# Recurrence heads of a two-block layer: the next head's first exponential and mixed operands made at the end of a head, and a longer first projection

## The reference, cut to what matters

```python
def hgrn2_forget(f_raw, lb):
    f = lb + (1 - lb) * jax.nn.sigmoid(f_raw.astype(jnp.float32))
    return jnp.log(f), 1 - f

def step(s, inp):                       # hgrn2_chunk_scan, over chunks of tokens
    qc, kc, vc, gc = inp
    gcum = jnp.cumsum(gc, axis=2)
    decay = jnp.exp(jnp.where(causal[:, :, None],
                              gcum[:, :, :, None, :] - gcum[:, :, None, :, :], -jnp.inf))
    att = jnp.einsum('bhtd,bhtsd,bhsd->bhts', qc, decay, kc)
    glast = gcum[:, :, -1:, :]
    o = (jnp.einsum('bhts,bhsv->bhtv', att, vc)
         + jnp.einsum('bhtd,bhdv->bhtv', qc * jnp.exp(gcum), s))
    s = (jnp.exp(glast[:, :, 0, :, None]) * s
         + jnp.einsum('bhsd,bhsv->bhdv', kc * jnp.exp(glast - gcum), vc))
    return s, o

# token_mix: q = silu(q); o = rms_norm(o_f + flip(o_b), hg_norm_w) * silu(og)
```

## Time and profile before

| What | Value |
|---|---|
| median of three runs | 4368.85 us |
| profiled execution | 4368.09 us, its span 4366.3 us |
| TensorE busy | 3848.4 us, 88% of the span |
| VectorE busy | 2488.9 us, 57% |
| ScalarE busy | 1522.4 us, 35% |
| GpSimd busy | 873.7 us, 20% |
| mean granted TensorE clock | 0.942 of full speed |

### The profile page before, as it was taken

One profiled execution on the slowest core, in us unless ns is written; L12 is line 12 of the kernel. 1 busy time (PEld: TensorE's weight loads), 2 busy tenths in 40 slices (PEclk: granted clock), 3 DMA queues, 4 the chain that ended last, 5 costly groups with the idle time before them and its releaser, 6 DMA issues. The chain is left out here.

```text
span 4366.3 us, 50841 instructions
## 1 busy us (share of the span) xinstructions
PE 3848.4 (88%) x19207; PEld 3090.7 (71%) x19207; DVE 2488.9 (57%) x4067; ACT 1522.4 (35%) x2294; POOL 873.7 (20%) x445
## 2 busy tenths in 40 slices
PE   6989989978999588888889979979799999999995
PEld 3768966448888577776645538867688788888884
DVE  2647860137777377777710038999755454545454
ACT  3424321034555244455510023346522232323231
POOL 0220002003333011111111004422144221212120
PEclk8989999989999789999989989989999999999997
DMA  4111003311110111111032323325655333333331
GB/s 179 42 39 36 24 20 111 133 70 39 49 44 30 41 39 40 45 48 39 25 149 87 125 88 111 116 96 189 211 205 194 132 124 118 125 115 128 112 131 47
DMA packets 135463, 403.35 MB, mean 92 GB/s; under 512 B 16369, under 2 KB 55137, under 8 KB 125665
## 3 DMA queue, kind: packets, MB, share of 16 engines
q1 hardware_dynamic: 135264, 400.68, 26.6%
HBM read 348.18 MB, written 52.45 MB: 92 GB/s over the span
## 5 line engine op out<-in xcount | busy, mean ns | idle before, releaser
L2654 POOL TENSOR_TENSOR ex_vl<-ex_v,ex_vh 128x1024 fp32r<-128x1024 f32 x80 | 191.9, 2399 | 685.7 <-ACT ex_vh L2642 685.7
L2638 ACT ACTIVATE ex_ab<-ps 128x512 f32<-128x512 f32 x80 | 47.8, 598 | 611.3 <-PE ps L346 611.3
L344 PE MATMUL ps<-ex_xh,ex_ul 128*128 128x512 f32 x640 | 250.1, 391 | 9.8 <-DVE ex_ul L2661 9.8
L344 PE MATMUL ps<-hT_high,ma_wl 128*128 128x384 f32 (+1 forms) x576 | 233.7, 406 | 24.9 <-DVE ma_wl L3599 24.9
L2680 DVE TENSOR_TENSOR ex_acc<-ex_acc,ps 128x512 f32<-128x512 f32 x160 | 109.8, 688 | 248.0 <-PE ps L346 248.0
L1822 DVE TENSOR_TENSOR mg_sg<-mg_sg,ps 128x512 f32<-128x512 f32 x32 | 22.0, 688 | 399.8 <-PE ps L1771 365.4
L346 PE MATMUL ps<-ex_xh,ex_uh 128*128 128x512 f32 x640 | 249.7, 390 | 0.0
L345 PE MATMUL ps<-ex_xl,ex_uh 128*128 128x512 f32 x640 | 249.7, 390 | 0.0
L344 PE MATMUL ps<-ex_vh,ex_al 128*128 128x512 f32 x640 | 249.0, 389 | 0.0
L345 PE MATMUL ps<-ex_vl,ex_ah 128*128 128x512 f32 x640 | 249.0, 389 | 0.0
L346 PE MATMUL ps<-ex_vh,ex_ah 128*128 128x512 f32 x640 | 249.0, 389 | 0.0
(11 more groups left out here) (539 smaller groups left out, 10401.1 us busy)
## 6 DMA issues: line engine op xcount, KB each, us to landing
ex_u<-in_peer_u SPq DMA_DIRECT2D x80, 512.0 KB, 4.2
ex_v<-in_peer_v SPq DMA_DIRECT2D x80, 512.0 KB, 4.1
gates_by_expert<-sg_gbuf SPq DMA_DIRECT2D x8, 4096.0 KB, 15.1
ma_w<-in_w_in_ma SPq DMA_DIRECT2D x48, 512.0 KB, 3.6
ev_v<-in_peer_v SPq DMA_DIRECT2D x48, 512.0 KB, 3.5
hg_w<-in_w_in_hg SPq DMA_DIRECT2D x40, 512.0 KB, 3.5
ex_g<-gates_by_expert SPq DMA_DIRECT2D x20, 1024.0 KB, 4.8
mg_wg<-in_w_merge SPq DMA_DIRECT2D x16, 1024.0 KB, 4.9
```

The costliest lines, as they stand in the source:

```text
L344: pe.matmul(out, a[1], b[0], start=start, stop=False)
L2638: act.activation(ab[:, j % 2, :], ps[:, j % 2, :], ACT.Gelu).then_inc(h_read, 1)
L2654: pool.tensor_tensor(vl[:, j], v[:, j % 2], vh[:, j].bitcast(F32), ALU.subtract).then_inc(vl_ready, 1)
```

## The change

TensorE makes 72 steps of projection ahead of the first head in place of 64. The loop's `fill` counts stay, so from there on every lot comes 8 steps earlier against the places, and the projection runs out 8 steps earlier. ScalarE's exponential of level 1 leaves place 1 and stands ahead of the loop for the first head and in place 13 of the head before for the others. VectorE's `mixed` of level 1 leaves place 1 and stands behind `weighted(0, 0)` for the first head and in place 14 of the head before, behind `low`, for the others.

```diff
-                fill(64)
+                fill(72)
                 for h in range(H):
...
+                def near(h, lv):
+                    i = level_of(h, lv)
+                    act.wait_ge(diff_ready, i)
+                    act.activation(dec[:, (i - 1) % DEC], dec[:, (i - 1) % DEC], ACT.Exp).then_inc(dec_ready, 1)
+
+                near(0, 1)
                 for h in range(H):
                     m, n, last = 8 * (h + 1), 5 * (h + 1), h + 1 == H
                     for at in range(1, 2 * LV + 1):
-                        for lv in (1, 2) if at == 1 else (at + 1,) if at < LV else ():
-                            i = level_of(h, lv)
-                            act.wait_ge(diff_ready, i)
-                            act.activation(dec[:, (i - 1) % DEC], dec[:, (i - 1) % DEC], ACT.Exp).then_inc(dec_ready, 1)
+                        if at < LV:
+                            near(h, at + 1)
...
                             evict(m + 6)
+                        if at == 13 and not last:
+                            near(h + 1, 1)
                         if at == 14 and not last:
                             high(n + 5 + FF)
...
                 weighted(0, 0)
+                mixed(0, 1)
                 for h in range(H):
                     n, last = 5 * (h + 1), h + 1 == H
                     for at in range(1, 2 * LV + 1):
-                        if at <= LV:
+                        if 1 < at <= LV:
                             mixed(h, at)
...
                         if at == 14:
                             low(n + 5 + FF)
+                            if not last:
+                                mixed(h + 1, 1)
```

## The result

The changed kernel takes 4337.83 us (median of 4 runs, 4337.45 to 4340.98), the kernel before 4369.06 beside it (4 runs, 4368.73 to 4370.84): ratio 0.9929 [0.9914, 0.9945]. That is 31.2 us less. The direction came out, the size did not.

A forecast was written before the change was run, and what follows sets the result against it. The prediction took each head as bound by TensorE except at its border, where a chain through the other engines holds it. Opening 0.4, six borders 9.9 and last border 5.6 gave 15.9 us off: 4353.0 us, range 4340 to 4366.

The forecast's parts named there:

- The scans' advance: At the border, with lots 8 steps ahead, the scan starts at 1332.7 instead of 1338.32, 5.6 us earlier.
- low(FF) at 1.47 us against 1.5: VectorE's cast of FF's second weight tile at the border takes 1.5 us, between bounds of 1.22 and 2.06.
- TensorE's arrival: At the border TensorE ends G's 8 steps at 1341.0, then waits 3.6 us before FF's steps.
- the wait's new place: TensorE's border wait now stands before an FF step, released by low(FF), not before the first level product; near 3.6 us.
- ScalarE's 5.65 us wait: ScalarE's wait for TensorE before copying the last projected FB tile, forecast to be gone.
- The gain of the last border: Before head 7, with no projection behind it, the whole chain comes earlier: gain 5.6 us, bounds 4.0 and 6.0.
- Rival 1: TensorE hangs on low(FF), queued behind the exponential; with no advance of the scans 24 us slower, 4392 us; chance 0.14.
- The turns of VectorE and GpSimd: Sharing SBUF's port pair, each blocks the other for a whole instruction; used to estimate low(FF) at the border.
- the slow clock: TensorE's 1.2 GHz after border waits, 1.7 us each, taken as equal before and after the change: zero gain.
- rival 3: The clock stays up through a 3.6 us wait: 10 us more gain, 4343 us, down to 4338; chance 0.12.
- The borders' 9.9: First level product at 1349.7 instead of 1351.31: gain 1.65 us at each of six borders, 9.9 us.
- The opening: Before the first level products, which start at 1000.0 instead of 1000.37: gain 0.4 us, bounds -1.5 and 1.3.

The follow-up runs named there:

- the two moves alone: Changed kernel with the first projection back at 64 steps, exponential and mixed pair still moved: 4371.19 us, ratio 1.0006 to the kernel before.
- The filler experiment: Kernel before, with 20 matmuls of 512 columns, result unread, in TensorE's wait at each border and in the opening: 4358.29 us, ratio 0.9976.
- those of the longer head: Changed kernel with 4 or 8 filler matmuls ahead of lot Q, heads 0.93 or 1.87 us longer: 4357.17 and 4355.82 us.
- the seven fillers: Changed kernel with 4 matmuls of 512 columns (0.93 us) ahead of each next head's lot Q: 4357.17 us, ratio 0.9971.
- removing the wait: Longer projection without the two moves, high(FF) and low(FF) moved to place 12: 4319.65 us, ratio 0.9886 to the kernel before.
- filling it: Longer projection without the two moves, plus 8 filler matmuls ahead of FF's steps: 4329.76 us, ratio 0.9907 to the kernel before.

## Why the prediction was off

**Where the 31.2 us are.** Measured from start to start of the second group of level products of each head: the opening gives 1.1 us (1006.86 to 1005.77), the six borders 21.8 (349.67 to 327.91 for six heads), the last one 5.9 (55.07 to 49.19), head 7 behind it nothing; 28.7 in all, and the last matmul of the stage has moved by as much. The span is 30.4 us shorter. The other 1.7 us lie behind the stage, in work that the change doesn't touch. From TensorE's long wait for proj_wl (end at 1457.04 before, 1428.43 after) to the end of the span it is 2909.3 us before and 2907.5 after, and in the profiles of the experiments 2906.7 to 2910.5. So the 1.7 us are no more than executions differ by. The last 0.8 us lie between the profiled executions and the medians.

**Right: the way.** The scans' advance (11.21 us behind the products against 11.3), low(FF) at 1.47 us against 1.5, TensorE's arrival 19.87 us after the group against 19.6, the wait's new place, and ScalarE's 5.65 us wait for the last FB copy gone. Its wait for the V copy is 1.54 us in place of 4.13, and the 4.17 us before the copy of Q are new, but both end before the chain needs them. The gain of the last border (5.9 against 5.6) rests on the advance alone and came out. Rival 1, 4392 us, needed an advance under 3.95 us; it was 5.9: 17.78 - 11.21, less 0.70 us by which products(7) comes later in the head. (The prediction had five steps of Q at 0.175 us, 0.9 us; four would give the 0.70.) The turns of VectorE and GpSimd held as I used them, also where the order of the two was changed by itself (the two moves alone).

**Wrong: the slow clock.** The step that failed is "The slow clock I put equal on both sides ... I take zero", 0 for a term that was 9.8 us. Before, the two groups behind the wait took 6.25, 5.76, 5.34, 5.37, 5.28 and 5.22 us at the six borders, against 3.65 at 2.4 GHz: 11.3 us lost. After, FF's steps lost 1.5 us at the first border and nothing at the others. The price itself was read about rightly (1.7 us a border and a microsecond more in the early heads; measured 1.57 to 2.60). What failed is that it would still be paid after the change, on FF's steps. What happened is rival 3, with a chance of 0.12 (forecast for it 4343 us, down to 4338). I had weighed it against one row, the wait of 3.90 us in the earlier trace rows, as though a wait a little shorter must cost the same. The filler experiment shows that the 11 us were there to be had in the kernel before, and those of the longer head show that keeping them isn't a matter of the wait's length alone. An even weight for 0 and for rival 3 would have been the honest reading.

**Small: the border and the opening.** The wait is 3.05 us for 3.6. Not all of that is gain: TensorE arrived 19.87 us behind the group for 19.6, and a later arrival shortens the wait but no head. What counts is low(FF), which ended 22.9 us behind the group for 23.2, less the 0.1 us by which FF's steps were longer than forecast. From products(7) to the next head's first level product it is 28.1 us where the clock held, for 28.3. With products(7) itself 0.70 us later for 0.88, that makes 0.34 us a border, 2.0 us in six. The borders' 9.9, the clock's 9.8 and these 2.0 give 21.7 us, where 21.8 are measured. The opening gave 1.1 us for 0.4, and by two errors that nearly cancel, both of the clock. FF's steps took 6.26 us there for 4.16, so the first level product came at 1002.12 for 1000.0; but the group behind it took 3.65 us, where the slow clock had made it 6.49 before (1000.37 to 1006.86).

**What each part does.** The lot of 8 steps gives the gain. The two moves give nothing by themselves; with the lot they lengthen the wait from 2.05 to 3.05 us, and yet the changed kernel is no slower than the lot alone (4337.83 and 4339.78, with ranges that overlap), as it loses the clock at one border and not at five. That is luck of the moves and not their design: 0.93 us more elsewhere in each head makes the kernel 19.3 us slower, of which the seven fillers themselves are 6.5. Of the 15.3 us by which the forecast missed, 9.8 are this luck.

**Open.** What in time decides whether TensorE keeps 2.4 GHz over such a wait. Waits of 3.96 us and more always lost it at these borders; 1.98 and 2.05 us lost it at five of six, 3.05 us held it at five of six, and lost it at five of six when the head was 0.93 or 1.87 us longer. The Trainium skill, "TensorE: Matmul & The Clock Gate", section "HAM oscillation — how this bites in real kernels", warns of idle gaps over a certain length. The runs here agree for 3.96 us and more; below that they show that the length of a gap is not enough to tell.

## What to carry to other kernels

In a software-pipelined stage, look which projection lot feeds the longest chain through the other engines and start that one a lot earlier; then make the operands of the lot that now stands at the border before that chain, not behind it, or it takes over the wait. Count what TensorE's clock costs behind each wait by itself, comparing the same instructions with and without the wait ahead of them, and give a kept clock a real chance when a change shortens a wait. Here a result that hung on waits of 2 to 3 us turned with a microsecond elsewhere in the loop; removing the wait (51.23 us a head) or filling it (53.54 us) took that chance out.

## What the runs showed of the hardware

Unexpected was that the clock depends on more than the wait: 3.04 us of idle was followed by 4.29 or by 6.88 us for the same 24 matmuls, in one and the same execution. A wait of 1.98 or 2.05 us could be followed by a loss, and at some borders the clock fell only when TensorE was at work again. And 20 and 8 filler matmuls in a wait, whose results nobody reads, were worth 10.8 and 10.0 us in the two kernels in which they stood in the wait.
